# Eight more gate tiles per projection move from the scan's second loop into the prompt attention: three tiles per head in twelve units

## What is computed

```python
def decoder_layer(x, p, pos, past, lam_init, g_mix, w_in, ...):
    h = rmsnorm(x, g_mix)
    z = h @ w_in                       # 2048 -> 8192 columns: q | k | v | u | gate_a | gate_s
    ...
    gate_a = jax.nn.sigmoid(z[..., U_END:U_END + D_MODEL])
    gate_s = jax.nn.sigmoid(z[..., U_END + D_MODEL:])
    q = partial_rope(rmsnorm(q, g_q), pos)
    k = partial_rope(rmsnorm(k, g_k), pos)
    att = diff_attention(q, pos, segments, lam)      # 8 heads, two softmax maps per head
    ...
    y_ssm, h_re, h_im = s5_scan(u, h0, ...)          # 64 groups, complex diagonal state
    ...
    x = x + (gate_a * branch_a + gate_s * branch_s) @ w_out
```

## Time and profile before

| what | value |
|---|---|
| median of 3 runs | 5338.01 us (5332.07 to 5351.67) |
| the profiled execution | 5345.69 us, of which its span is 5343.9 us |
| PE matmul busy in the span | 4848.2 us (91%) |
| mean granted clock of PE | 0.946 of full speed |
| end of the scan's first loop, end of its second, on PE | 727.4 us and 830.1 us |
| the eight heads, from the first scores to the last values | 990.0 us to 1350.8 us |

### The profile page before, as it was taken

One profiled execution on the slowest core, in us unless ns is written; L12 is line 12 of the kernel. 1 busy time (PEld: TensorE's weight loads), 2 busy tenths in 40 slices (PEclk: granted clock), 3 DMA queues, 4 the chain that ended last, 5 costly groups with the idle time before them and its releaser, 6 DMA issues. The chain is left out here.

```text
span 5343.9 us, 82357 instructions
## 1 busy us (share of the span) xinstructions
PE 4848.2 (91%) x28806; PEld 4443.5 (83%) x28806; DVE 2413.3 (45%) x4202; ACT 1598.4 (30%) x2467; POOL 2503.2 (47%) x1751
## 2 busy tenths in 40 slices
PE   4899996688895997989989999999799999999979
PEld 3888895577332997989879999999799999999879
DVE  4366631456003211067757733444355555565421
ACT  2222221344002322232225533333333333333232
POOL 3277750122000443334664467777555656565433
PEclk7999996799897998999999999999899999999989
DMA  2233330222751444223335589999877777777423
GB/s 77 75 88 89 87 102 17 72 88 84 278 213 49 133 134 136 72 76 97 99 106 186 188 283 324 323 319 321 279 274 279 265 280 271 272 279 264 172 85 95
DMA packets 351218, 925.89 MB, mean 173 GB/s; under 512 B 41426, under 2 KB 118738, under 8 KB 300146
## 3 DMA queue, kind: packets, MB, share of 16 engines
q1 hardware_dynamic: 279090, 570.85, 33.3%
q0 software_dynamic: 37872, 272.25, 13.4%
q10 hardware_dynamic: 34128, 81.15, 4.0%
HBM read 838.10 MB, written 86.02 MB: 173 GB/s over the span
## 5 line engine op out<-in xcount | busy, mean ns | idle before, releaser
L2477 PE MATMUL val_y_ps<-val_wt,val_v 128*128 128x416 f32 x6144 | 1183.7, 353 | 29.9 <-POOL val_v L2462 29.9
L2477 PEld LDWEIGHTS val_y_ps<-val_wt,val_v 128*128 128x128 f32 x6144 | 1141.7, 188 | 71.9 <-issue 30.2
L239 PE MATMUL rt_acc<-xn_act,rt_w_hi 128*128 128x416 f32 x4096 | 1130.2, 357 | 33.9 <-POOL rt_w_rest L229 33.7
L229 POOL TENSOR_TENSOR rt_w_rest<-rt_w_raw,rt_w_hi 128x512 fp32r<-128x512 f32 x576 | 760.0, 1335 | 628.9 <-ACT rt_w_hi L224 625.4
L2462 POOL TENSOR_TENSOR val_v<-val_v_raw,val_v 128x2048 fp32r<-128x2048 f32 x128 | 592.2, 4627 | 464.8 <-ACT val_v L2508 464.8
L239 PEld LDWEIGHTS rt_acc<-xn_act,rt_w_hi 128*128 128x128 f32 x4096 | 764.9, 190 | 51.9 <-issue 23.1
L239 PE MATMUL rt_acc<-xn_act,rt_w_rest 128*128 128x416 f32 x2048 | 718.5, 351 | 0.0
L2558 DVE TENSOR_TENSOR out_xT<-out_xT,val_y_ps 128x416 f32<-128x416 f32 x512 | 299.5, 585 | 488.6 <-PE val_y_ps L2477 460.9
L224 ACT ACTIVATE rt_w_hi<-rt_w_raw 128x512 fp32r<-128x512 f32 x576 | 348.3, 629 | 543.0 <-DMA rt_w_raw<-in_peer_uT 346.8
L2384 DVE CUSTOM_DVE_ANT_0 rt_space<-rt_space,rt_mid 128x2048 f32<-128x2048 f32 x128 | 292.8, 2288 | 457.5 <-DMA rt_space<-in_peer_u,out_row_id 455.2
L2508 ACT ACTIVATE val_v<-val_v_raw 128x2048 fp32r<-128x2048 f32 x128 | 245.7, 1919 | 626.3 <-PE val_y_ps L2477 624.9
(11 more groups left out here) (400 smaller groups left out, 7728.2 us busy)
## 6 DMA issues: line engine op xcount, KB each, us to landing
rt_w_raw<-in_peer_uT SPq DMA_DIRECT2D x512, 256.0 KB
val_v_raw<-in_peer_vp SPq DMA_DIRECT2D x128, 1024.0 KB, 5.0
scan_w_raw<-in_w_in SPq DMA_DIRECT2D x160, 256.0 KB, 3.1
pages_K<-in_cache_kT SPq DMA_DIRECT2D x64, 512.0 KB
pages_V<-in_cache_v SPq DMA_DIRECT2D x64, 512.0 KB, 5.8
hid_scratch<-rt_hid ACTq DMA_DIRECT2D x128, 208.0 KB
gate_scratch<-rt_space ACTq DMA_DIRECT2D x13, 2048.0 KB, 7.3
val_hid<-hid_scratch SPq DMA_DIRECT2D x32, 832.0 KB
```

Of the source, the lines that this page charges most:

```text
L229: e.tensor_tensor(self.rest[:, s, 0:nk, :], self.raw[:, s, 0:nk, :], self.hi[:, s, 0:nk, :].bitcast(F32), ALU.subtract).then_inc(self.rest ...
L239: mm = e.matmul(acc[:, h, 0:width], w[:, s, k, :], act[:, kt0 + k, a, col + h * width:col + (h + 1) * width], start=first and k == 0 and w ...
L2477: mm = e.matmul(y_ps[:, t % 2, 0:DW], v[:, c % 2, a, j, t * P:(t + 1) * P], wt[:, g % 2, j, b, :], start=j == 0 and a == 0 and b == 0, sto ...
```

## The change

The second loop of the scan is taken out, on all engines. Its 8 gate tiles go to the prompt attention, which now computes 24 gate tiles, three per head, in twelve units (HEAD = 3U). The staging tile `zout` there gets a third buffer and a third semaphore. SP loads four more units per head, POOL does four more subtractions, and PE and ACT have the new units and copies written in at chosen places; `gate_hi(3)` moves ahead of `exponents(0)`, and the copy out of the first tile moves ahead of `copy_weights(1)`.

```diff
@@ stage_scan
-        PER1, PER2 = 4 * U, 2 * U
-        N1, N2 = CT, (KT - CT) // 2
-        BASE2 = N1 * PER1
+        PER1 = 4 * U
+        N1 = CT
...
             body1(N1 - 1, last=True)
-            for u in range(U - 1):
-                w.split_hi(e, 0, PER2, BASE2 + u)
-            evacuate(N1 - 1, 3, False)
-            w.split_hi(e, 0, PER2, BASE2 + U - 1)
+            evacuate(N1 - 1, 3)
             finish_y(N1 - 1)
-            for u in range(U, 2 * U):
-                w.split_hi(e, 0, PER2, BASE2 + u)
-            evacuate(0, 0, True)
-            with e.Fori(1, N2) as i:
-                body2(i, False)
-            evacuate(N2 - 1, 1, True)
...
             body(N1 - 1, last=True)
-            gates(0, first=True)
-            with e.Fori(1, N2) as i:
-                gates(i)
+            respond(N1 - 1, 3)
@@ stage_attention_prompt
-        zout = s.sb("zout", [P, 2, TOK])
+        zout = s.sb("zout", [P, 3, TOK])
...
-        HEAD, PER = 2 * U, 4 * U
-        FIRST_GATE = 3 * NH + CT + KT
+        HEAD, PER = 3 * U, 6 * U
+        FIRST_GATE = 3 * NH + CT + CT
...
-                gate_tiles(i, s, range(RING, RING + 2))
+                gate_tiles(i, s, range(RING, RING + 3))
                 store_values(i, s)
                 load(i, s + 1, 2)
-                gate_tiles(i, s, range(RING + 2, RING + HEAD))
+                gate_tiles(i, s, range(RING + 3, RING + HEAD))
@@ stage_attention_prompt, PE, both()
                 gate_unit(i, s, 0)
                 if with_norm:
                     squares(i, s + 1, 0)
+                gate_unit(i, s, 1)
 
                 scores(i, s, 1)
-                gate_unit(i, s, 1)
+                gate_unit(i, s, 2)
                 if with_norm:
                     rotate(i, s + 1, 0)
                 turn_weights(i, s, 0)
-                gate_unit(i, s, 2)
+                gate_unit(i, s, 3)
                 values(i, s, 0)
 
                 scores(i, s, 2)
                 if with_norm:
                     squares(i, s + 1, 1)
-                gate_unit(i, s, 3)
+                gate_unit(i, s, 4)
+                gate_unit(i, s, 5)
                 turn_weights(i, s, 1)
+                gate_unit(i, s, 6)
                 values(i, s, 1)
 
                 scores(i, s, 3)
-                gate_unit(i, s, 4)
+                gate_unit(i, s, 7)
                 if with_norm:
                     rotate(i, s + 1, 1)
                 turn_weights(i, s, 2)
-                gate_unit(i, s, 5)
+                gate_unit(i, s, 8)
                 values(i, s, 2)
 
-                gate_unit(i, s, 6)
+                gate_unit(i, s, 9)
                 turn_weights(i, s, 3)
-                gate_unit(i, s, 7)
+                gate_unit(i, s, 10)
+                gate_unit(i, s, 11)
                 values(i, s, 3)
```

More of the change, by code:

```diff
@@ L617, in column1, with z_row @@
             return i * 3 + q if q < 3 else i + GATES
-        def z_row(i, a, second):
-            if second:
-                return i * 2 + (24 + CT + a)
+        def z_row(i, a):
             return i * 3 + a if a < 3 else i + 24
@@ L628, in _ @@
                     w.load(e, i, PER1, u, columns(k.w_in, column1(i, u // U), UNIT * (u % U)))
[L629 to L632, removed]
         @block.gpsimd
@@ L666, in _ @@
             ch.end(N1)
-            with e.Fori(0, N2) as i:
-                for u in range(PER2):
-                    w.split_rest(e, i, PER2, BASE2 + u)
         @block.vector
@@ L718, in _, with evacuate @@
             e.wait_ge(zero_done, 8)
-            def evacuate(i, t, second):
+            def evacuate(i, t):
                 a = t % 2
[L723 to L729, removed]
+                w.wait_used(e, i, PER1, (t + 1) * U)
+                e.wait_ge(z_stored[a], i * 32 + 16 * (t // 2 + 1))
+                e.activation(halves(zout[:, a, :]), acc[:, :, 0:HALF], ACT.Copy).then_inc(evac, 1)
+                e.wait_ge(evac, i * 4 + (t + 1))
                 e.sem_inc(acc_free, 1)
-                e.dma_start(k.z_dram[ds(z_row(i, t, second), 1)].rearrange("o p n -> p (o n)"),
+                e.dma_start(k.z_dram[ds(z_row(i, t), 1)].rearrange("o p n -> p (o n)"),
                             zout[:, a, :]).then_inc(z_stored[a], 16)
@@ L749, in body1 @@
                     if q:
-                        evacuate(i, q - 1, False)
+                        evacuate(i, q - 1)
                     elif not first:
-                        evacuate(i - 1, 3, False)
+                        evacuate(i - 1, 3)
                     w.split_hi(e, i, PER1, q * U + U - 1)
@@ L766, in finish_y @@
                 e.dma_start(k.y_dram[ds(i, 1), :, 0:NP].rearrange("o p n -> p (o n)"), yout[:]).then_inc(y_stored, 16)
[L768 to L775, removed]
             stage(0, 0)
@@ L781, in _ @@
             body1(N1 - 1, last=True)
-            for u in range(U - 1):
-                w.split_hi(e, 0, PER2, BASE2 + u)
-            evacuate(N1 - 1, 3, False)
-            w.split_hi(e, 0, PER2, BASE2 + U - 1)
+            evacuate(N1 - 1, 3)
             finish_y(N1 - 1)
-            for u in range(U, 2 * U):
-                w.split_hi(e, 0, PER2, BASE2 + u)
-            evacuate(0, 0, True)
-            with e.Fori(1, N2) as i:
-                body2(i, False)
-            evacuate(N2 - 1, 1, True)
             for a in range(2):
-                e.wait_ge(z_stored[a], 16 * (2 * N1 + N2 + 1))
+                e.wait_ge(z_stored[a], 16 * (2 * N1 + 1))
             e.wait_ge(y_stored, 16 * (N1 + 1))
@@ L832, in body @@
                         w.multiply(e, i, PER1, q * U + u, acc, k.act, u * UNIT, u == 0, u == U - 1)
[L834 to L843, removed]
             drive(0, 0)
@@ L1066, in stage_attention_prompt @@
         chain_sem = s.sem("chain")
-        acc_free, evac, z_stored = s.sem("acc_free"), s.sem("evac"), s.sems("z_stored", 2)
+        acc_free, evac, z_stored = s.sem("acc_free"), s.sem("evac"), s.sems("z_stored", 3)
         block = s.block()
         U = KT // UNIT
-        HEAD, PER = 2 * U, 4 * U
-        FIRST_GATE = 3 * NH + CT + KT
+        HEAD, PER = 3 * U, 6 * U
+        FIRST_GATE = 3 * NH + CT + CT
         SCALE = DK ** -0.5
@@ L1112, in gate_tiles @@
                         w.load(e, i, PER, s * HEAD + u,
-                               columns(k.w_in, i * 4 + (FIRST_GATE + (s * HEAD + u) // U), UNIT * (u % U)))
+                               columns(k.w_in, i * 6 + (FIRST_GATE + (s * HEAD + u) // U), UNIT * (u % U)))
             def load(i, s, j):
@@ L1178, in gate_unit @@
                 if u % U == 0:
-                    e.wait_ge(acc_free, at(i, s, 2, u // U + 1))
+                    e.wait_ge(acc_free, at(i, s, 3, u // U + 1))
                 w.multiply(e, i, PER, s * HEAD + u, acc, k.act, (u % U) * UNIT, u % U == 0, u % U == U - 1)
@@ L1283, in _ @@
             e.sem_inc(acc_free, 1)
-            e.sem_inc(z_stored[0], 16)
-            e.sem_inc(z_stored[1], 16)
+            for t in range(3):
+                e.sem_inc(z_stored[t], 16)
             def gate_hi(i, s, u):
@@ L1293, in gate_out @@
                 e.activation(halves(zout[:, t, :]), acc[:, :, 0:HALF], ACT.Copy).then_inc(evac, 1)
-                e.wait_ge(evac, at(i, s, 2, t + 1))
+                e.wait_ge(evac, at(i, s, 3, t + 1))
                 e.sem_inc(acc_free, 1)
-                e.dma_start(k.z_dram[ds(i * 4 + (FIRST_GATE - CT + 2 * s + t), 1)].rearrange("o p n -> p (o n)"),
+                e.dma_start(k.z_dram[ds(i * 6 + (FIRST_GATE - CT + 3 * s + t), 1)].rearrange("o p n -> p (o n)"),
                             zout[:, t, :]).then_inc(z_stored[t], 16)
@@ L1340, in both @@
                 gate_hi(i, s, 2)
+                gate_hi(i, s, 3)
                 exponents(i, s, 0)
@@ L1343, in both @@
                     deviation(i, s + 1, 0)
-                gate_hi(i, s, 3)
+                gate_hi(i, s, 4)
                 copy_weights(i, s, 0)
@@ L1348, in both @@
                     square(i, s + 1, 1)
-                gate_hi(i, s, 4)
+                gate_hi(i, s, 5)
                 exponents(i, s, 1)
-                gate_hi(i, s, 5)
+                gate_out(i, s, 0)
+                gate_hi(i, s, 6)
+                gate_hi(i, s, 7)
                 copy_weights(i, s, 1)
-                gate_out(i, s, 0)
                 exponents(i, s, 2)
@@ L1357, in both @@
                     deviation(i, s + 1, 1)
-                gate_hi(i, s, 6)
+                gate_hi(i, s, 8)
+                gate_hi(i, s, 9)
+                gate_out(i, s, 1)
                 copy_weights(i, s, 2)
-                gate_hi(i, s, 7)
                 exponents(i, s, 3)
-                if with_norm:
-                    gate_hi(i, s, 8)
+                gate_hi(i, s, 10)
+                gate_hi(i, s, 11)
                 copy_weights(i, s, 3)
                 if with_norm:
-                    gate_hi(i, s, 9)
+                    gate_hi(i, s, 12)
+                    gate_hi(i, s, 13)
```

(4 more changed lines are left out.)

## The result

The changed kernel takes 5285.84 us (median of 6 runs, 5280.52 to 5293.69) where the kernel before takes 5347.49 (median of its 6 runs by then): a ratio of 0.989 with a 95% interval of 0.9873 to 0.9908, that is, faster by 49 to 68 us. That forecast and measurement meet within 2 us is partly luck: the six runs of before have a median 9.5 us above that of the first three, and the saving is about 8 us larger than forecast, and the two nearly cancel.

A forecast was written before the change was run, and what follows sets the result against it. PE bounds the scan's second loop; in the heads it is busy 307 of 360.8 us, with gaps. Scan -100.0, heads 6.2 + 13.3 + 24.1 + 7.0 - 4.5 = +46.1, net -53.9: 5284 us, range 5270 to 5300.

The forecast's parts named there:

- Gone from the scan: End of the scan: without its second loop the next stage's first load comes 100.0 us earlier.
- Unit 1: Ahead of a head's second scores: first rotation +0.6 us in three slow heads, +1.1 in four fast; +6.2 us.
- Units 2 and 3: On both sides of turn_weights(1): second squares to second rotation 15.6 us instead of 13.7; +13.3 us over 7 heads.
- Unit 4: Between turn_weights(3) and the last values, where nothing waits: 3.01 us in full, +24.1 us over 8 heads.
- What stays: Between turn_weights(2) and turn_weights(3) the 0.86 us wait stays; the third tile's accumulator hand-over and the added loads cost nothing.
- The last head: Head without rotations: first two added units 3.0 us each, the third +1.0; together +7.0 us, the fourth counted separately.
- The clock: In the heads, granted clock 0.95 on average: filling the gaps gives -4.5 us, ends 0 and -18.
- DVE blocked by POOL: Rival in the heads: 32 added subtractions at 1.29 us each on the last chain, +41 us, 5325 us; chance 0.07.
- The gaps move instead of filling: Rival in the heads: each chain starts later by what PE got, all 96.3 us return, 5334 us; chance 0.07.
- The clock back whole: Rival in the heads: the clock gives back 18 us instead of 4.5, 5270 us; chance 0.07.
- PE at its lower clock: Rival in the heads: PE falls to its lower clock, whole stage 335 us more, about 5620 us; chance 0.03.
- The signs that were named: First load near 734; heads 51, 52 us; stretch 400 to 410, PE over 95%; waits under 6, under 4, near 7.

The follow-up runs named there:

- the second profile of before: The unchanged kernel before, run once more on the experiments' chip for its profile: 5342.63 us, the heads 358.1 us.
- the fastest kernel: Changed kernel with unit 5 behind turn_weights(1), gate_hi(5) behind exponents(1) and gate_hi(3) behind deviation(0): 5262.11 us, 0.9846 of the kernel before.

## Why the prediction was right, by its own steps

- **Gone from the scan**, predicted 100.0: 100.07 in the trace, 98.8 in total by itself. Both pieces that were put on the path behind the last tile, y's copy and its store, took what the rows of before gave them.
- **Unit 1**, predicted +0.6 in the slow form of the head and +1.1 in the fast: in the slow form the rotation moved from 12.99 us behind the head's start to 13.51, +0.5; in the fast one from 11.29 to 12.29, +1.0. That `gate_hi(3)` adds to the chain was shown: with it moved back, the slow form's 0.44 us wait is gone.
- **Units 2 and 3**, predicted +1.9: 13.7 to 15.5, +1.8, with ACT's and DVE's chain ending last by 0.31 us, as worked out (8.1 against 7.9).
- **Unit 4**, predicted +3.01 in full: from `turn_weights(3)` to the next head it is 7.50 us instead of 4.49.
- **What stays**: the wait ahead of `turn_weights(3)` was predicted at 0.86 and is 0.93. The accumulator's hand-over for the third tile, costed at nothing, is hidden in the seven heads that norm a successor, but not in the last, where no rotation covers it:

```profile
1279.79 0.77 PE L239 MATMUL att_acc<-in_act,att_w_hi 128*128 128x272 f32 x4 [0.43 <-ACTq L1255]
```

  From `turn_weights(2)` to `turn_weights(3)` that head takes 7.72 us where it took 7.03, so the missing cover costs 0.7 us, once. Where all added units stood in a row it was 0.76 us in a head. No wait for a load stands in PE's lists.
- **The last head**, predicted +10.0 with unit 4: 44.89 us against 34.47 in the second profile of before, which had no slow matmuls there, so +10.4. Unit 3 cost 0.7 and not 1.0, and the hand-over the 0.7 that the sum did not have.
- **The clock**, predicted -4.5 with ends 0 and -18: the granted clock rose from 0.95 to 0.99. The steps above come to about 49 us (5.5 + 12.3 + 24.1 + 0.5 + 7.0 for the last head), the stretch grew by 43.9 against one profile of before and by 46.6 against the other, so by difference the clock gave back 3 to 5.5. Not all of that is the clock: from the first rotation to the second squares the fast heads take 5.80 us and not 6.04, 1 us over four of them, though the rows between run at full speed in both; and the last head's extra 0.4 goes the other way. So the clock's own part is about 2 to 5 us. In the rows it is plain: in the first profile of before, the fast head from 1130.62 took 46.02 us and the one from 1224.74 took 45.10, and behind the first rotation four matmuls of a unit took

```profile
1144.35 1.11 PE L239 MATMUL att_acc<-in_act,att_w_hi 128*128 128x272 f32 x4
```

  in the one and 0.66 in the other (1238.04). The last head has 1.5 us of it in that profile (35.97) and none in the second (34.47). The four fast heads of the changed kernel all take 50.6 to 50.7. The prediction tied the slow rotation to the longest gap; the head from 1176.64 had a gap of 2.53 us as well, and there the rotation took 1.18 us and the matmuls behind it were the slow ones. The lower level at the start of the heads is in both kernels (0.87 in the first 14 us before, 0.83 in 16 us after) and was not the change's to win.
- **The rivals.** DVE blocked by POOL: the mechanism exists, and costs 8.0 to 8.6 us of the stretch by the run with short subtractions, all of it in the one wait that the forecast already held. Here is that place in the changed kernel's timeline, first POOL:

```profile
1084.55 2.53 POOL L229 TENSOR_TENSOR att_w_rest<-att_w_raw,att_w_hi 128x512 fp32r<-128x512 f32 x2 [7.33 <-ACT att_w_hi L224]
```

And DVE:

```profile
1084.96 0.89 DVE L1388 TENSOR_TENSOR att_stat<-att_stat,heads_neg_lam 128x1 f32<-128x1 f32 x1
1085.77 1.59 DVE L1389 TENSOR_SCALAR att_e_buf<-att_e_buf,att_stat 128x512 f32<-128x512 f32 x1
1087.39 0.75 DVE L1390 SCALAR_TENSOR_TENSOR att_e_buf<-att_e_buf,att_stat 128x512 f32<-128x512 f32 x1
```

  Two subtractions in a row hold DVE's two steps to their ends: 0.89 for 0.16 us, 1.59 for 0.48. The Trainium skill, "SBUF — State Buffer", section "SBUF: two separate sides", describes this as an exclusive lock that the later of the two waits out in full; these rows agree: the pair's middle is at 1085.82 and its end at 1087.08, and the two steps end at 1085.85 and 1087.36. Of the second step, which has one tile and a column for its inputs, the section says this only in a two-port mode; no run tells the mode. It doesn't follow that each lock costs time: the other pairs of subtractions in that head began at 1049.16, 1064.09, 1074.68 and 1090.16, while DVE was idle, worked on the scores' bounds, took the reciprocal, or was idle again, and stretched nothing; a single one at 1059.92 stretched DVE's sum for the rotated q from 0.72 to 1.07 us, and the exponents that the next steps need ended about as late anyway.
- **The gaps move instead of filling**: not so, and the row of units in one place shows what that would have looked like, 1.000.
- **The clock back whole, and PE at its lower clock**: neither. The clock gave 2 to 5 us and not 18, and the granted clock in the heads rose.
- **The signs that were named**: the next stage's first load at 732.29, with the whole execution 1.7 us ahead; heads of 50.7 and 52.1 us; the stretch at 404.7, PE busy for 96% of it; the three waits at 3.0, 3.7 and 8.6 us.
- **The total**: -53.9 predicted, -60.5 and -61.7 by the medians. The heads and the scan together give -53 to -56, well inside the interval of 49 to 68; the rest is within what the part behind the heads varies by itself from one execution to another; whether a few microseconds of it are the change's own is not shown. That the profiled span fell by 64 is for 8 us that part.

## What to carry to other kernels

Work moved to a stage whose engine already holds it for 85% of the time is free only as far as it stands in that engine's gaps, and behind the instruction that starts the chain which ends the gap: the same 32 units cost 103 us in one place of a head, 44 in four places, 28 once the second chain was started before the filler, and 23 with ACT's two copies out of the chains as well. So walk each gap as two sums, the filler's and the chain's, and take out of the chain whatever other engines do on the way there. An engine that is far from busy (POOL, 30% of this stage) can still be in a chain through what it blocks, and only where it meets it.

## What the runs showed that was not expected

A wait of PE costs more than its idle time. Three waits of 1.54 us together, taken out, gave 2.24 us a head, and one of 0.93 gave 1.15 (50.73 to 49.58); the matmuls right behind a wait took 1.18 instead of 1.08 us and 0.55 instead of 0.49. One wait of 0.53 gave 0.53 (48.48 to 47.95), so it isn't the same everywhere.

The starts of the rows say where the rest comes from. The view counts idle time from the modelled end of the instruction before, and in an unbroken stream the next row starts ahead of that end. With unit 5 moved, the second rotation starts 0.24 us behind the start of a row that is 0.41 long:

```profile
1073.96 0.41 PE L239 MATMUL att_acc<-in_act,att_w_rest 128*128 128x272 f32 x2
1074.20 1.08 PE L1151 MATMUL att_ss<-att_normed,all_const 128*128 128x272 f32 x4
```

In the changed kernel the same two starts are 0.72 us apart (the rotation is the row at 1078.54 above):

```profile
1077.82 0.41 PE L239 MATMUL att_acc<-in_act,att_w_rest 128*128 128x272 f32 x2
```

So 0.48 us went for 0.31 of idle. By the same count of starts, the third block's weights lost 0.57 for 0.30 and the fourth's 1.09 for 0.93, and the unit behind each 0.05 more: together 2.24. Ahead of the third scores there was no overlap to lose: in the fastest kernel they start 0.39 us behind the start of a row of 0.38, and with the wait 0.92 behind it, which is 0.53 for 0.53. To price a wait, compare the distance of two starts with and without it, and not its idle time. The ends being modelled, what the engine does in the overlap is not shown.
